# Two-layer attention and expert trunk on one core: odd-batch memory laid out by last use, three more 1 MB loads during the mixer, packed latent heads, second norm's scale applied by column, input rows first in the queue

## What is computed

```
for l in range(DEPTH):
    mix = hybrid_mixer(x, w_in[l], q_norm[l], w_uq[l], kv_norm[l], w_ukv[l], w_out[l])
    x = layer_norm(ALPHA * x + mix, ln1_g[l], ln1_b[l])
    ffn = moe_ffn(x, router_w, router_b, moe_w1[l], moe_w3[l], moe_w2[l])
    x = layer_norm(ALPHA * x + ffn, ln2_g[l], ln2_b[l])
```

## Time and profile before

| | us |
|---|---|
| median of 3 runs | 1198.99 (1198.69 to 1200.06) |
| the profiled execution | 1200.85 |
| its span, first to last instruction | 1198.7 |
| PE busy | 1080.9 (90%) |
| DVE, ACT, POOL busy | 370.2, 192.7, 30.1 |
| mean granted clock of PE | 0.986 |

### The profile page before, as it was taken

The page is one execution under the profiler, slowest core; times in us unless marked ns, Lnnn a source line. Parts: engine busy times, 40 slices in busy tenths (PEclk is TensorE's granted clock), DMA queues, the critical chain, the costliest instruction groups (busy, mean ns, idle before and its releaser), DMA issues.

```text
span 1198.7 us, 16350 instructions
## 1 busy us (share of the span) xinstructions
PE 1080.9 (90%) x6112; PEld 602.4 (50%) x6112; DVE 370.2 (31%) x997; ACT 192.7 (16%) x460; POOL 30.1 (3%) x44
## 2 busy tenths in 40 slices
PE   8999999989999888888899999989989889988886
PEld 5565565444455444444455655544455544444443
DVE  1244462222232222222342445422223222222224
ACT  1144221111111110101012342111111111100100
POOL 0001010000000000000000100100000000000000
PEclk9999999999999998989999999999999999998999
DMA  9863589999999999999988437999999999999996
GB/s 360 336 220 142 211 351 418 421 423 420 423 421 423 422 422 422 423 421 421 395 305 318 156 124 280 379 420 423 421 423 422 422 422 421 423 422 422 422 421 232
DMA packets 83457, 442.67 MB, mean 369 GB/s; under 512 B 9696, under 2 KB 25184, under 8 KB 35296
## 3 DMA queue, kind: packets, MB, share of 16 engines
q1 hardware_dynamic: 82848, 440.53, 90.4%
q10 hardware_dynamic: 432, 1.11, 0.2%
q0 software_dynamic: 144, 0.58, 0.1%
HBM read 441.15 MB, written 1.05 MB: 369 GB/s over the span
## 4 chain that ended last, share of the span: by engine, by line
PE 47%; SPq 44%; issue 3%; DVE 2%; DMA 2%; ACT 2%; DVEq 0%; ACTq 0%
SPq L331 26%; SPq L335 13%; PE bank L555 12%; PE bank L817 7%; PE bank L836 6%; PE bank L625 5%; SPq L418 4%; PE bank L868 4%; PE bank L873 3%; DMA w_odd<-in_moe_w 2%; PE bank L788 1%; PE bank L843 1%; PE bank L595 1%; ACT w_odd L1262 1%; PE bank L610 1%
## 5 line engine op out<-in xcount | busy, mean ns | idle before, releaser
L817 PE MATMUL bank<-moe,x 128*128 128x128 f32 x960 | 232.9, 402 | 0.0
L817 PEld LDWEIGHTS bank<-moe,x 128*128 128x128 f32 x960 | 230.7, 334 | 0.0
L1262 ACT ACTIVATE moe<-bank 128x512 f32<-128x512 f32 (+2 forms) x190 | 101.4, 543 | 752.4 <-PE bank L836 358.4
L555 PE MATMUL bank<-w_odd 128*128 128x384 f32 (+1 forms) x448 | 150.7, 493 | 2.8 <-ACT w_odd L1262 2.8
L873 PE MATMUL bank<-moe 128*128 128x512 f32 x256 | 118.4, 605 | 24.1 <-DVE moe L1227 24.1
L836 PE MATMUL bank<-w_odd,moe 128*32 128x512 f32 x1024 | 119.4, 612 | 14.4 <-DMA w_odd<-in_moe_w 14.4
L836 PE MATMUL bank<-w_even,moe 128*32 128x512 f32 x1024 | 116.8, 603 | 12.1 <-DMA w_even<-in_moe_w 9.9
L1201 DVE COPY moe<-bank 128x512 f32<-128x512 f32 x64 | 44.3, 692 | 243.8 <-PE bank L836 243.5
L555 PEld LDWEIGHTS bank<-w_odd 128*128 128x128 f32 x448 | 84.0, 190 | 61.7 <-issue 11.2
L873 PEld LDWEIGHTS bank<-moe 128*128 128x128 f32 x256 | 46.0, 189 | 99.0 <-DVE moe L1227 51.4
L836 PEld LDWEIGHTS bank<-w_odd,moe 128*32 128x32 f32 x1024 | 31.1, 111 | 96.4 <-issue 75.7
(11 more groups left out here) (150 smaller groups left out, 685.8 us busy)
## 6 DMA issues: line engine op xcount, KB each, us to landing
w_even<-in_moe_w SPq DMA_DIRECT2D x192, 1024.0 KB, 25.7
w_odd<-in_moe_w SPq DMA_DIRECT2D x184, 1024.0 KB, 26.3
w_odd<-in_w_in SPq DMA_DIRECT2D x12, 1536.0 KB, 7.6
w_odd<-in_w_out SPq DMA_DIRECT2D x4, 2048.0 KB, 7.6
w_odd<-in_moe_w SPq DMA_DIRECT2D x16, 512.0 KB, 16.6
w_odd<-in_w_in SPq DMA_DIRECT2D x4, 832.0 KB, 11.0
w_odd<-in_ln_g SPq DMA_DIRECT2D x4, 512.0 KB, 7.9
w_odd<-in_ln_b SPq DMA_DIRECT2D x4, 512.0 KB, 10.3
```

The lines of the kernel that those rows point to most:

```text
L555: last = mm(h_bank[b][t][:, 0:n], xT[:, c, t * P:(t + 1) * P], w[:, c, :], start=c == 0, stop=c == DC - 1)
L817: last = mm(bank[2 + c // 4][:, c % 4 * P:(c % 4 + 1) * P], xc[:, t, c, :], chosen[:, t, :], start=t == 0, stop=t == 1)
L1262: return fn(dst, src, ACT.Copy)
```

## The change

- **Odd buffer.** The mixer's tensors are placed by the moment of their last use. Slot 3 of w13 holds the latent q and k, q and k of the first six heads and the latent v; `load_w13(1, 3, 1)` leaves after ten scores (`s_psum`, 10), `load_w2(1, 2, 1)` after the last turn (`ropT_psum`, 8), both ahead of the w_out halves in SP's queue. `nrm[0]` moves to other memory, and the wait for `first_gathered` goes.
- **w_in and x by halves.** xT's column groups are ordered (h, p, c) with h of 2: each half of x's columns gives four groups. Each w_in block loads in two transfers.
- **Start.** x tile 0 is first in SP's queue, tile 1 behind the first w_in block; the constants wait for the whole block. `keep_warm(12)` becomes `keep_warm(3)`. DVE copies column groups 0 to 3 of both tiles, ACT 4 to 7; the projection waits for each half alone.
- **Latent heads packed.** q and k latents keep the 64 plain columns of a pair of heads in one 128-row block and the 32 rotated columns of all four in a third: 3 transposes per tile where 4 were, and `latent_scores`: per head a 64-row and a 32-row product that add up. All four heads are scored at once, between the two halves of block 4's projection.
- **Second norm.** ACT writes (Y - mean) * rstd as x, in halves; PE transposes this, and the copies to xT apply g and b as scale and bias per partition (`n2_cols`, two small loads more per layer). DVE multiplies and adds g and b to the rows later (`finish_rows`). `keep_warm(16)` becomes `keep_warm(4)`, and goes after layer 1. There DVE, ACT and POOL share the quarters of x, stored one by one.
- **Last batch.** The second half of `down` runs expert by expert, each behind its own transfer.

The core of the diff:

```diff
@@ sync
+            sp.dma_start(x[:, 0, :], x_in[:, 0, :]).then_inc(x_loaded[0].sem, 16)
...
                 stream_item(0)
+                if l == 0:
+                    sp.dma_start(x[:, 1, :], x_in[:, 1, :]).then_inc(x_loaded[1].sem, 16)
                 stream_item(1)
...
                 load_ln(sp, l, 0)
+
+                after(sp, l, s_psum, 10)
+                load_w13(1, 3, 1)
+                after(sp, l, ropT_psum, 8)
+                load_w2(1, 2, 1)
                 load_w_out(0)
                 load_w_out(1)
...
                 after(sp, l, o_psum, PAIRS)
                 load_w13(1, 2, 1)
-                load_w13(1, 3, 1)
...
                 load_w2(1, 0, 1)
-                after(sp, l, first_gathered, 1)
-                load_w2(1, 2, 1)
@@ tensor, project
                         for c in range(DC):
+                            if b == 0 and c == 0:
+                                after(pe, l, xT_dve, 3 if t else 1)
+                                if l and t == 0:
+                                    after(pe, l, xT_act, 1)
                             if b == 0 and c == DC // 2:
+                                after(pe, l, xT_act, 3 if t else 2)
+                                if l and t == 0:
+                                    after(pe, l, xT_dve, 2)
@@ tensor
+                def latent_scores():
+                    after(pe, l, h_act, 4)
+                    after(pe, l, upT_sb, 4)
+                    for q_cols, k_cols in ((slice(0, P), slice(0, P)), (slice(P, SEQ), slice(0, SEQ))):
+                        out_cols = slice(q_cols.start, q_cols.start + k_cols.stop)
+                        for h in range(MLA_HEADS):
+                            rows = slice(64 * (h % 2), 64 * (h % 2) + 64)
+                            mm(score_bank[h][:, out_cols], qaT[rows, h // 2, q_cols], kaT[rows, h // 2, k_cols],
+                               start=True, stop=False)
+                        for h in range(MLA_HEADS):
+                            rows = slice(32 * h, 32 * h + 32)
+                            last = mm(score_bank[h][:, out_cols], qaT[rows, 2, q_cols], kaT[rows, 2, k_cols],
+                                      start=False, stop=True, tile_position=(32 * h, 0))
+                            if q_cols.start:
+                                last.then_inc(s_psum.sem, 1)
@@ tensor, last batch
+                        for k in range(NB):
+                            pe.wait_ge(w2_in[parity][k].sem, (b0 + j) * 8 + 16)
+                            for c in range(2):
+                                last = mm(bank[3][BLK * k:BLK * (k + 1), :], hT[:, c, BLK * k:BLK * (k + 1)],
+                                          w2_slots[parity][k][:, c, 512:1024], start=c == 0, stop=c == 1)
+                        last.then_inc(y2_psum.sem, 1)
@@ vector, copy_xT
+                    if l == 0:
+                        after(v, l, xT_psum, 2 * t + 1)
+                        nc.vector.tensor_copy(xT[:, 0:4, t * P:(t + 1) * P],
+                                              bank[2 * t][:, :].rearrange("p (c t) -> p c t", c=4)
+                                              ).then_inc(xT_dve.sem, 2 - t)
+                        return
+                    for h, cols in ((0, (0, 1)), (1, (0, 1))) if t == 0 else ((0, (0, 1, 2, 3)),):
+                        after(v, l, xT_psum, 2 * t + h + 1)
+                        for c in cols:
+                            last = ts(xT[:, 4 * h + c, t * P:(t + 1) * P], bank[2 * h if t == 0 else 2][:, c * P:(c + 1) * P],
+                                      n2_cols[:, 0, 4 * h + c:4 * h + c + 1], n2_cols[:, 1, 4 * h + c:4 * h + c + 1],
+                                      ALU.mult, ALU.add)
+                        last.then_inc(xT_dve.sem, 1)
@@ vector, end of a layer
+                moments(0, 6, LN_EPS / ALPHA ** 2)
+                if l == DEPTH - 1:
+                    center(1, 0, lambda h: Y[0][h][:, :], (0,))
+                after(v, l, y_half, 2)
+                nc.vector.bn_stats(stats[:, 1, 0, :], Y[1][0][:, :])
+                deviation(0)
+                v.wait_ge(y_added.sem, b1 * NT + 2)
+                link(nc.vector.bn_stats(stats[:, 1, 1, :], Y[1][1][:, :]))
+                moments(1, 7, LN_EPS / ALPHA ** 2)
+                if l < DEPTH - 1:
+                    deviation(1)
+                else:
+                    center(1, 1, lambda h: Y[1][h][:, :])
+                    stretch(1, 1, out_dve)
+                    stretch(1, 0, out_dve, (0,))
@@ scalar
+                def normalise(l, t, halves=(0, 1)):
+                    after(act, l, shift_ok, t + 1)
+                    for h in halves:
+                        fn(x[:, t, h * 512:(h + 1) * 512], Y[t][h][:, :], ACT.Identity,
+                           scale=rstd[:, 6 + t:7 + t], bias=shift[:, t:t + 1]).then_inc(n2_ready.sem, 1)
```

262 lines of the change are left out of this document (144 added, 118 removed).

## The result

The changed kernel is slower by half a per cent: 1205.94 us, median of 5 runs (1204.23 to 1206.57), against 1198.99 before (5 runs, 1198.26 to 1200.46). The ratio is 1.0052, with a 95% interval from 1.0038 to 1.0067. The forecast was 1196.6 us, the range ended at 1202.5. The profiled execution took 1206.57 us with a span of 1204.6, so 5.9 us of span stand against the earlier trace rows, whose execution spanned 1198.7.

The account below looks back on a forecast made before the run. Full transfer engines in the expert stretches, so start, mixer, layer boundary and tail set the time; +2.85 - 2.8 + 0.4 - 1.6 + 0 - 1.2 = -2.35 us, forecast 1196.6 us, range 1192.5 to 1202.5.

Parts of the forecast that it names:

- The 3 MB at 0: Three early 1 MB transfers per layer, ahead of the first release: worth 0, as the queue was empty there.
- The start at +2.85: Kernel start: later first projection +0.9, cold clock +2.25, more evenly split copies of tile 1 -0.3; together +2.85 us.
- 2.8 MB lie up to and with tile 1: Start, SP's queue: at 404 GB/s tile 1 lands about 10.2 us, PE starts at 11.3, +0.9 us.
- 5.5 us of it gives 2.8, the 3.3 us give 1.7, I take the middle: Start, first projection: part runs at 1.2 GHz, costing +2.25 us (bounds 0 and 2.8).
- Rival B: Start: the clock is already up when the projection starts, 1194.3 us; chance 0.14.
- The mixer at -1.4 per layer: Mixer: fewer transposes and filled waits -1.2, packed latent scores -0.3; about -1.4 us per layer, -2.8 in all.
- 0.1 for each of five changes of shape: Mixer, latent scores on PE: 0.1 us per change between row shapes, within 2.4 us of scores against 2.7.
- w_out at +0.4: Mixer's end: w_out half 0 lands at 112.9 us behind w2(1,2), wanted at 112.79; +0.2 us per layer.
- The boundary at -1.6: Layer boundary: PE's first projection 2.0 us earlier, tile 1's DVE copies +0.4; -1.6 us (bounds -1.0, -2.1).
- The last batch at 0: Last expert batch, second product: starts 0.4 us earlier, but the last expert's data lands when it did; 0.
- The tail at -1.2: After the last transfer: DVE, ACT and POOL share four quarters, last store issued at 1194.7; -1.2 us (bounds -0.6, -1.6).
- From there on the bytes per layer are fixed, so a layer's end moves exactly as its first release moves: Expert stream after the first release: its length does not change, so no term was given.

Follow-up runs that it names:

- Experiments 4 and 5: Changed kernel with w_out's first half issued ahead of w2(1,2), 1203.63 us; changed kernel with the three 1 MB transfers back at their old queue places, 1204.21 us.
- Experiment 2: Changed kernel with 24 keep-warm passes at the start instead of 6, DVE still waiting for both tiles: 1207.88 us, ratio 1.0058.
- experiment 9: Kernel before with only the last batch's second product reordered, all four passes of one expert's strip together: 1199.28 us, ratio 1.0002.
- the last version: Changed kernel with early DVE start, filled pause, w_out order, tail addition on DVE, slots at 512, third w_in block ahead of w13(0,1): 1180.67 us, ratio 0.9843.
- experiment 3: Changed kernel with DVE's first wait for tile 0 alone and four keep-warm passes between tile 0's transposes and the first projection: 1200.36 us, ratio 1.0011.

## Why the prediction was wrong

**The 3 MB at 0: right.** Experiments 4 and 5 give the same time, and transfers idle ahead of the release even where the 3 MB come late.

**The start at +2.85: the mechanism was right, both sizes were off.** The step that failed first is "2.8 MB lie up to and with tile 1 ... with the landing about 10.2": tile 1 landed at 11.9. Its two terms were both too good: the transfer engines had moved 0.73 MB by 5 us, not 0.89, and ran at 366 GB/s up to 10 us, not at 404; and by the landing they had moved 3.3 MB, so about 0.5 MB of what stands behind tile 1 in the queue moved with it. That makes the first projection 2.6 us late instead of 0.9. The second is the clock, "5.5 us of it gives 2.8, the 3.3 us give 1.7, I take the middle": it was 5.5 us at the lower level and cost 2.65. I took the middle of two ends of which one was plainly the nearer, an engine coming up after idling at the start. I had given two reasons together, six passes in place of 24 and nearly 5 us of idle time behind them. Experiment 2 takes them apart: it restored the 24 and gained nothing, so with that pause the first reason counted for nothing. Rival B (1194.3) fell with the first projection's slow passes.

**The mixer at -1.4 per layer: right mechanism, -0.98 measured.** The part up to the projection was right within 0.1 us. The term that was mis-sized is "0.1 for each of five changes of shape": each took about 0.2, and the gain fell short by 0.4 us per layer. The row for it was there: in the earlier trace rows the change to 64 rows costs 0.09 us ahead of L583, which I counted, and 0.1 more inside it, where two rounds take 0.32 in place of 0.21. I wrote "with the change of shape" beside the 0.32 and then left this part out of the price.

The Trainium skill (TensorEngine Tiling (Array Packing), Tiling Modes) says that a change of mode drains the array. The Trainium skill gives no price for it. I had put a pass's tail, 0.3 us, on it; the 0.2 us measured lie midway between that and my 0.1, and no row here shows a drain as such. They do not come from products that add up in one bank either: the step from 32 rows back to 64, which starts new sums, costs the same.

**w_out at +0.4: +1.98 measured.** The step "0.8 if it queues behind something more" was too narrow, and I had used one layer's picture for both. The half landed 5.4 us behind w2(1,2) in layer 0, as forecast, but 6.8 in layer 1 (and 6.9 in layer 0 of experiment 2). Why these differ stays open; the cure is the same.

**The boundary at -1.6: -1.88 measured**, -2.3 to the first projection and +0.4 to the second, both as forecast.

**The last batch at 0: right** (experiment 9).

**The tail at -1.2: -0.14 measured.** The step that failed is "stretch 2 x 0.7 and 0.7" beside "POOL: 1.25 + 1.25": I costed each engine alone and set them side by side. Here they did not run side by side while both read two tensors from SBUF. DVE's centring, which reads PSUM and one tensor, stands beside POOL's product at 1197.3 us with its usual 0.74.

The Trainium skill (SBUF — State Buffer, Who interferes with whom) says just that: a VectorE operation with two SBUF inputs contends with a GpSimd operation that reads SBUF, over a pair of ports that works as an exclusive lock. The trace agrees, with 1.05 and 1.75 us for operations of 0.75; which of the two waits at which moment its rows do not show.

**The term that was missing: 2.9 us in the traces for the stream.** "From there on the bytes per layer are fixed, so a layer's end moves exactly as its first release moves" is the sentence that failed. The bytes were fixed, their rate was not: the diff lengthened a small tensor by 64 bytes per partition, and I read that line without asking what lies behind it.

By the rates alone it is about 1.5 us per layer, by the two traces 1.64 and 1.26.

With the measured sizes in place of mine the sum is 5.1 - 2.0 + 2.0 - 1.9 + 0 - 0.1 + 2.9 = +6.0, against 5.9 between the two spans.

## What to carry to other kernels

In a kernel that is bound by its transfers, look at the addresses of what they fill before anything else: here starting them 160 bytes earlier, at a multiple of 256, was worth 12 us in the kernel before, more than the 6.8 us that everything else in the last version gained over it. When one engine's copy moves to another, read what that engine's program waits for ahead of it, even where the wait has nothing to do with the copy. And after each wait that goes, look for the next one in the trace: the filled pause gained nothing in the whole (experiment 3), and the wait that had taken its place went only when the block of w_in was moved too.
